# Halved weight splits between evacuations in the memory and second value projections, and residual additions ahead of the split in the residual projections

## The reference

```python
proj = h @ w_in                                 # second block; va and vb are columns of it
k, v = jnp.split(mem_n @ w_kv, 2, axis=-1)      # memory: 256 rows, w_kv 1024 x 2048
...
x = x + _hybrid_mixer(...)                      # ends in: merged @ w_o
x = x + _memory_cross_attention(...)            # ends in: o @ w_o
x = x + _sq_relu_mlp(...)
```

## Time and profile before

| | |
|---|---|
| median of 3 runs | 1726.62 us (1724.86 to 1727.92) |
| span of the profiled execution (the time that the profile gives for it) | 1727.8 us |
| TensorE busy | 1685.5 us, 98% |
| VectorE, ScalarE, GpSimd busy | 884.8, 772.0, 631.1 us |
| MKV on TensorE | 787.9 to 839.9 us |
| V2 on TensorE | 847.3 to 892.1 us |
| granted TensorE clock in both | 1.00 of full speed |

### The profile page before, as it was taken

How to read it: one execution, slowest core, us unless ns; L and a number is a source line. 1 busy time by engine, 2 the same in 40 slices (tenths; PEclk the granted TensorE clock), 3 DMA queues, 4 the chain that set the end, 5 groups by cost and what they waited for, 6 DMA issues and landing times. The chain is left out here.

```text
span 1727.8 us, 27062 instructions
## 1 busy us (share of the span) xinstructions
PE 1685.5 (98%) x10190; PEld 1431.6 (83%) x10190; DVE 884.8 (51%) x1554; ACT 772.0 (45%) x1366; POOL 631.1 (37%) x439
## 2 busy tenths in 40 slices
PE   7999999999999999999999999999999999999998
PEld 6987777778888889988997788798787788989896
DVE  4223333344445328947645565687544575555552
ACT  5324554532223334556545655444445324626251
POOL 1007665633330076742103422866200227414242
PEclk9999999999999999999999999999999999999999
DMA  7231221223334223243731111223511223222221
GB/s 318 100 96 37 73 79 49 73 104 121 109 111 146 98 73 118 103 162 134 290 130 65 52 47 50 85 104 133 216 50 50 98 73 114 107 98 97 97 98 49
DMA packets 29800, 181.65 MB, mean 105 GB/s; under 512 B 3352, under 2 KB 5784, under 8 KB 10112
## 3 DMA queue, kind: packets, MB, share of 16 engines
q1 hardware_dynamic: 22136, 150.12, 24.0%
q10 hardware_dynamic: 7560, 30.09, 4.9%
HBM read 169.57 MB, written 10.50 MB: 104 GB/s over the span
## 5 line engine op out<-in xcount | busy, mean ns | idle before, releaser
L409 PE MATMUL acc<-rarena,wh 128*128 128x512 f32 (+1 forms) x1720 | 659.1, 383 | 10.5 <-DVE farena L1863 2.8
L410 PE MATMUL acc<-rarena,wh 128*128 128x512 f32 (+1 forms) x1720 | 643.7, 374 | 0.0
L411 PE MATMUL acc<-rarena,wl 128*128 128x512 f32 (+1 forms) x1720 | 643.5, 374 | 0.0
L409 PEld LDWEIGHTS acc<-rarena,wh 128*128 128x128 f32 x1720 | 324.7, 189 | 91.9 <-issue 26.7
L411 PEld LDWEIGHTS acc<-rarena,wl 128*128 128x128 f32 x1720 | 324.6, 189 | 62.8
L410 PEld LDWEIGHTS acc<-rarena,wh 128*128 128x128 f32 x1720 | 324.9, 189 | 56.8 <-issue 0.5
L312 DVE TENSOR_TENSOR wl<-raw,wh 128x2048 fp32r<-128x2048 f32 x85 | 207.0, 2435 | 259.5 <-ACT wh L306 259.4
L306 ACT ACTIVATE wh<-raw 128x2048 fp32r<-128x2048 f32 x103 | 196.5, 1908 | 76.2 <-PE acc L411 69.4
L312 POOL TENSOR_TENSOR wl<-raw,wh 128x2048 fp32r<-128x2048 f32 x18 | 82.6, 4586 | 153.2 <-ACT wh L306 153.2
L2495 POOL TENSOR_TENSOR wl<-raw,wh 128x512 fp32r<-128x512 f32 x78 | 104.9, 1373 | 91.5 <-ACT wh L1281 91.5
L487 PE MATMUL acc<-wh,rarena 128*128 128x256 f32 x384 | 109.1, 284 | 4.0 <-DVE rarena L1738 2.5
(11 more groups left out here) (320 smaller groups left out, 2904.2 us busy)
## 6 DMA issues: line engine op xcount, KB each, us to landing
raw<-in_w SPq DMA_DIRECT2D x129, 1024.0 KB, 4.8
early<-in_wmod SPq DMA_DIRECT2D x8, 1024.0 KB, 19.7
farena<-in_gate ACTq DMA_DIRECT2D x4, 1024.0 KB, 4.7
mkv_scratch<-rarena ACTq DMA_DIRECT2D x2, 2048.0 KB, 12.5
rarena<-mkv_scratch ACTq DMA_DIRECT2D x1, 4096.0 KB, 13.3
farena<-in_rpb ACTq DMA_DIRECT2D x16, 240.0 KB, 3.8
farena<-in_x_grid SPq DMA_DIRECT2D x2, 1024.0 KB, 8.0
o_scratch<-early ACTq DMA_DIRECT2D x8, 256.0 KB, 2.0
```

Source lines behind the costliest of these rows:

```text
L409: mm(o, w[0], m[0], start=start, stop=False)
L410: mm(o, w[0], m[1], start=False, stop=False)
L411: return mm(o, w[1], m[0], start=False, stop=stop)
```

## The change

In MKV, VectorE's split of job c+1 is two instructions over four k each: the first where the whole one stood, the second behind the low part of group t = 0. `lo_done` counts with the second. In V2, ScalarE's split is halved too (second half behind the evacuation of b = 0), and VectorE's halves stand ahead of the evacuations of b = 1 and b = 2; both of VectorE's wait for both of ScalarE's. In `stream`, used for WO2 and OM, the addition of group n comes first and the split behind it. No other projection is changed.

```diff
--- before.py
+++ after.py
@@ -313,6 +313,22 @@
                .then_inc(s_("lo_done"), 1)
 
 
+
+        def split_hi_half(act, base, n):
+
+            s, k = base % 2, slice(4 * n, 4 * n + 4)
+            act.wait_ge(s_(f"raw_loaded{s}"), half(0, 2, base) * 16 + 16)
+            ins = nc.scalar.activation(wh[:, s, k], raw[:, s, k], ACT.Copy)
+            if n == 1:
+                ins.then_inc(s_("hi_done"), 1)
+
+        def split_half(eng, base, n):
+
+            s, k = base % 2, slice(4 * n, 4 * n + 4)
+            eng.wait_ge(s_("hi_done"), base + 1)
+            ins = eng.tensor_tensor(wl[:, s, k], raw[:, s, k], wh[:, s, k].bitcast(f32), ALU.subtract)
+            if n == 1:
+                ins.then_inc(s_("lo_done"), 1)
 
         def acc_wait_free(pe, it, per, base):
             pe.wait_ge(s_(f"acc_free{base % 2}"), half(it, per, base) + 1)
@@ -1411,8 +1427,10 @@
             act.wait_ge(s_("spread_done"), 4)
             f(rstd, S[0][:], ACT.Copy).then_inc(s_("rstd_ready"), 1)
             for c in range(4):
-                split_hi(act, 0, 2, JB["V2"] + c + 1)
+                split_hi_half(act, JB["V2"] + c + 1, 0)
                 for b in range(4):
+                    if b == 1:
+                        split_hi_half(act, JB["V2"] + c + 1, 1)
                     g = GB["V2"] + 4 * c + b
                     acc_wait_ready(act, 0, 2, g)
                     n = 128 if c < 2 else 64
@@ -2078,8 +2096,10 @@
 
             for c in range(8):
                 v.wait_ge(s_("lo_done"), JB["MKV"] + c + 1)
-                split_job(v, 0, 2, JB["MKV"] + c + 1)
+                split_half(nc.vector, JB["MKV"] + c + 1, 0)
                 for t in range(2):
+                    if t == 1:
+                        split_half(nc.vector, JB["MKV"] + c + 1, 1)
                     for k in X1_TILES.get(c, ())[t:t + 1]:
                         x1_tile(k)
                     g = GB["MKV"] + 2 * c + t
@@ -2108,8 +2128,9 @@
 
 
             for c in range(4):
-                split_job(v, 0, 2, JB["V2"] + c + 1)
                 for b in range(4):
+                    if b in (1, 2):
+                        split_half(nc.vector, JB["V2"] + c + 1, b - 1)
                     g = GB["V2"] + 4 * c + b
                     v.wait_ge(s_("v_hi"), 4 * c + b + 1)
                     n, t = 128 if c < 2 else 64, v2[:, b, 512 * c:512 * c + 512]
@@ -2262,10 +2283,10 @@
                 free_acc(tt(y[:, n], acc[g % 2][:], y[:, n], ADD), g)
 
             def stream(name, n, gain, made0):
+                g = GB[name] + n
+                add_stream(0, 2, g, n)
                 if n % 2 == 0 and (name, n) != ("WO2", 0):
                     split_job(v, 0, 2, JB[name] + n // 2 + 1)
-                g = GB[name] + n
-                add_stream(0, 2, g, n)
                 wait_evacuated(v, 0, 2, g)
                 v.wait_ge(s_("xg_hi"), made0 + n + 1)
                 stt(xg[1][:, n], y[:, n], vec(gain + n), xg[0][:, n].bitcast(f32), MUL, SUB).then_inc(s_("xg_ready"), 1)
```

## The result

| | median | range | executions |
|---|---|---|---|
| before | 1726.59 us | 1724.33 to 1729.56 | 18 |
| after | 1731.55 us | 1728.30 to 1734.31 | 18 |

The ratio is 1.0025 with a 95% interval of 1.0018 to 1.0032: the change makes the kernel slower by 0.25%, between 3.1 and 5.5 us. The forecast was 1727.0, its own range 1725.0 to 1729.0; the wide range, rivals included, ended at 1731.5. No measurable change was the likeliest case and did not come; what came is near the first rival.

The account below looks back on a forecast made before the run. TensorE, busy 98% of the span, was taken as the bound, with at most 6.4 us of waits to win. Terms +0.8 +0.4 -1.6 +0.3 +0.5 = +0.4 us gave about 1727.0, own range 1725.0 to 1729.0.

Parts of the forecast that it names:

- the wide range: Whole kernel: 1723.8 to 1731.5 us, rivals included, with all but about 15% inside.
- No measurable change: Whole kernel: time within 0.2% (3.5 us) of before, given 69%.
- the first rival: MKV: spill gets ahead of job 7's load, c = 7 starts 3.1 to 6.2 us late; 1729.8 to 1733, 18%.
- The step that failed: MKV: job 7's load goes out at 821.48, the spill at about 822.0, load first by 0.5 us; cost 0.
- the collision in c = 3: MKV: VectorE's second half meets GpSimd's second add and ends 0.8 us late; c = 4 starts 0.9 us late.
- the order of the chain itself: MKV: same instructions between high part and TensorE's start, in another order; gain 0.
- The lock's places: MKV c = 3 and c = 5: VectorE and GpSimd exclude each other on the port pair; FL about 0.8 us late.
- 1.4 was forecast: MKV: c = 6 starts 1.4 us late after the collisions with GpSimd.
- 1.6 forecast: V2 at c = 3: TensorE's whole wait before b = 2 goes, gain 1.6 us.
- 0.3 forecast: V2 at c = 1: second half copy delays the evacuation of b = 1, cost 0.3 us.
- V2's load was given 0.4 us: V2's job 1: load goes out behind the spill x_scratch and lands at 852.5, cost 0.4 us.
- The second rival: V2's start: load lands at 854 to 858, TensorE waits 2 to 6 us; 1728.6 to 1732.6, 20%.

Follow-up runs that it names:

- number 5: Kernel before, no split halved, first spill mkv_scratch issued some 3 us earlier, behind the high part of c = 4's group 0: 1728.92 us against 1727.09, ratio 1.0007.
- number 1: Only MKV's halved splits, V2 and stream as in the kernel before: 1731.15 us against 1727.36, ratio 1.0023.
- number 6: Changed kernel with the split in c = 4 of MKV whole again: 1732.46 us against 1727.09 for the kernel before, ratio 1.0038.
- 10: Kernel before with V2's halves for c = 0, 2, 3 and MKV's group 0 x1 tile behind its low part: 1726.93 us against 1727.46, ratio 0.9993.
- number 11: Kernel before with only MKV's x1 tile of group 0 moved behind its low part, all splits whole: 1729.17 us, ratio 1.0012.
- number 9: Changed kernel, MKV splits c = 4, 7 whole, GpSimd's second add in c = 3, 5 held for the half split: 1726.69 us against 1727.46 before, ratio 0.9994.
- number 4: Changed kernel with its first spill mkv_scratch issued 3 us later: 1735.33 us against 1727.36 for the kernel before, ratio 1.0043.
- 7: Changed kernel with MKV's splits in c = 4 and c = 7 whole again: 1728.63 us, ratio 1.0004 against the kernel before.
- 2: Only V2's halved splits, MKV and stream as in the kernel before: 1726.26 us against 1727.36, ratio 0.9995.
- 3: Only the addition ahead of the split in WO2 and OM, the rest as in the kernel before: 1729.57 us against 1727.36, ratio 1.0009.
- 8: Kernel before with V2's halves for c = 0, 2 and 3 only, c = 1 whole: 1725.37 us against 1727.09, ratio 0.9990.
- 12: As 10, with GpSimd's first add in c = 5 held and x_scratch issued behind the square root: 1726.07 us against 1727.08 before, ratio 1.0003.

## Why the prediction was right and wrong

**The step that failed** is "the load is still first, by 0.5 us ... I count 0 here". It failed twice. The load's time was right: 821.48 was forecast, and 817.70 is 821.5 on the clock of before (in this profile the stage begins 3.8 us earlier). The spill was forecast at 822.0 and left at 821.56, because the collision in c = 3 cost 0.4 us and not 0.8, so that c = 4 was 0.45 late and not 0.9. And a lead of 0.5 us would not have been worth 0. Leads and landings of a 1 MB load beside a 2 MB spill, from the traces of before, after and the experiments:

| load leads by | 2.97 | 2.43 | 1.98 | 1.23 | 0.80 | 0.60 | 0.06 | -0.16 | -0.29 | -0.37 | -0.72 | -0.80 |
|---|---|---|---|---|---|---|---|---|---|---|---|---|
| job 7, us | 4.7 | 5.2-5.3 | 5.3 | | 6.7 | | 9.4 | | | | | 9.2 |
| V2's job 1, us (a second spill follows) | | | | 6.3 | 6.5 | 6.7 | | 11.5 | 12.6 | 13.1 | 14.2 | |

(The columns are those that bear on the argument; the other traces lie on the same course.) For job 7 the landing grows from 5.1 to 5.6 us at a lead of 2 us to 6.7 at 0.80 and 9.4 at 0.06, and is no longer at -0.80. A lead of 0.5 us lies between the columns of 0.80 and 0.60 and that of 0.06: 7 to 8 us, an estimate, so a landing at 828.5 to 829.5 where 827.5 was needed.

How two transfers share depends on how far apart they leave. The queues of number 5 in 815 to 816 (spill issued at 813.33, load at 814.13) and of the changed kernel in 842 to 843 (load at 839.15, `x_scratch` at 839.75):

```profile
q10 hardware_dynamic: 16, 0.26, 66.5%
...
q1 hardware_dynamic: 31, 0.25, 78.9%
```

In each only one queue moves. In number 5 the load moved nothing before 818, when the spill had moved 1.6 of its 2 MB; in the changed kernel `x_scratch` moved nothing before 844, when the load was nearly through. Where the two leave 0.4 us apart or less (job 7's load in the changed kernel and number 1, V2's in 6, 10 and 11) they take turns after 2 to 4 us.

**The first rival** had the mechanism, a load that the spill slows down, at 18%. Its condition (a collision shorter than about 0.4 us) was met only just: the collision cost 0.40 us, and the spill left 0.06 us behind the load and not in front of it. Its picture, one transfer behind the whole of the other, is what number 5 shows at 0.80 us, and not what came at 0.06. The row on which it rested is weak: the load beside the spill had just been issued, and in the changed kernel too a load moves little in the first microsecond (0.03 MB in 818 to 819). The next microsecond bears it out: 0.02 MB for that load in 827 to 828, and 0.15 for an undisturbed one at the same age (820 to 821, both in the trace of before). The Trainium skill (DMA: Bandwidth & Descriptors, "Queues, rings and completion order") says that an engine goes round the queues at packet granularity; this trace agrees (16 packets of one, 17 of the other), and the prediction took from it more than it says, that the later transfer waits for the whole earlier one. In the first 4 us of number 5, where one queue moved alone, no such turns show.

The rival had c = 7 start 3.1 to 6.2 us late; the transfer made it 2.4, and 3.4 with the 1.0 that c = 6 was late. Its total of 1729.8 to 1733 holds the result. That the wide range of the prediction reaches to the edge of the result is owed to this rival at 18%, and not to the forecast's own sum.

**Right:** the order of the chain itself is worth 0 (number 9). The lock's places, c = 3 and c = 5, were right, its size by half in c = 3; the start of c = 6 was 1.0 us late, where 1.4 was forecast. The Trainium skill (SBUF — State Buffer, "SBUF: two separate sides") has the shared port pair held by one engine for the whole instruction; the traces agree, in that a half that starts inside an add is longer by about the add's rest (0.53 for 0.67 us in c = 5, 0.40 for 0.54 in c = 3) and is 1.22 us again when the add is moved. The whole split of number 11 shows 1.04 for 1.18, and the prediction's own rows 2.20 for 2.34, where it read 2.2 as all that was left: each time 0.14 us less than the rest. V2: 1.6 forecast, 1.75 measured; 0.3 forecast, 0.45 measured. OM: 0.5 and 0.5. WO2: 0 and 0.

**Wrong by cancelling:** V2's load was given 0.4 us for going out behind `x_scratch`. It left 0.60 us ahead of it, because the stop at c = 7 had delayed the spill, and cost nothing. The second rival (20%) is real: TensorE waited 4.0 us for it in number 4 and 2.6 in number 6, once that stop was gone.

**What stays open.** The stages in the traces add to +2.2 us by the waits and +2.5 by the starts, the times say +3.1 to +5.5. A fall of the clock behind a longer stop is a likely place for the rest. In the changed kernel's own profile it did not fall behind the stops at c = 6 and c = 7, and executions without a profile don't show where it falls. Their mean clock goes with their time: those with 0.990 or 0.991 took 1732.6 to 1734.3 us, those with 0.994 or 0.995 took 1728.3 to 1731.4; that goes together, and does not say which stage it comes from. In number 1 a fall at c = 6 was taken up by the wait at c = 7, so that alone would not make the sum larger.

## What to carry to other kernels

When an edit moves the event that releases a load, lay the load's new issue beside every other transfer of that stretch and price the lead: here 2 us were free, 0.06 us cost 4.1 us of landing and 2.4 us of TensorE, for a split whose own end was hidden. A wait that is removed may have been what kept a spill behind the next load; after each repair ask again which transfer now goes first. And take halves only where a whole one is waited for: V2's c = 3 gained 1.75 us, MKV's eight gained none.

## What the runs showed of the hardware

**A stop of 2 us can be followed by half clock, one of 1 us was not.** Ahead of c = 6, TensorE stopped 1.85 to 2.04 us in five kernels (the changed one, numbers 1, 4, 6, 7), and the granted clock fell from 1.00 to 0.50 behind it in four of them, for about 3 us, costing 1.4 to 1.6. In the nine with a stop of 1.1 us or less there (before, 2, 3, 5, 8 to 12) it never did. Elsewhere it fell behind a stop of 4.0 us (4, in V2) and one of 2.0 (12, ahead of FL), and not behind 2.5 us (the changed kernel), 2.6 (6) and 2.0 (11). So the 1.0 us that the collisions with GpSimd add to the stop ahead of c = 6 can cost 2.4.

**The clock of two single profiles hides the edit.** The profile of before ran at half clock at 44 us, where the changed kernel did not, and at full clock at 1171 us, where it did not. Before, then after, same windows:

```profile
44.00:45.00 1.00, 1.00 (x6) 1.00 (x6) 0.74 (x2) 1.00 (x4) 0.00 (x0) 0.50 0.00 0
1171.00:1172.00 1.00, 1.00 (x9) 1.00 (x10) 0.90 (x3) 1.00 (x3) 1.00 (x2) 1.00 0.00 0
```

```profile
44.00:45.00 1.00, 1.00 (x8) 1.00 (x9) 0.93 (x3) 0.81 (x2) 0.00 (x0) 1.00 0.00 0
1171.00:1172.00 1.00, 1.00 (x7) 1.00 (x6) 1.00 (x3) 0.28 (x1) 1.00 (x2) 0.50 0.00 0
```

The first made before 3.8 us later up to MKV (with the stretch behind 130 us), the second the changed kernel 1.4 us later again, of which 0.5 had come back by 1192 us; the code at both places is the same. Of the other traces all but numbers 4 and 8 show the second fall. Without both, the changed kernel's span would be some 2.8 us longer than that of before, close to the +2.5 of the stages. An execution's time is 1.7 us above its span (1729.41 and 1727.7 in the changed kernel's profile), so the profile of before is like an execution of 1729.5, 2.9 above its median, and that of the changed kernel is one of its five fastest of 18, 2.1 below its median: so the spans are equal while the medians are 5 us apart.
